# MoE layer: each token's expert outputs added up in one DRAM row by accumulating indirect stores, the last two experts' outputs kept on chip, and the order of the last products changed

## The chip, the cores and the metric

The kernel runs on one core of a Trainium2 chip. The metric is the device time of one execution in microseconds (us). The core has a matrix engine (TensorE, "PE" in the profile, its weight loads "PEld"), VectorE ("DVE"), ScalarE ("ACT"), GpSimd ("POOL") and SyncE ("SP"), which issues most of the transfers, and 16 DMA engines that carry them out.

## What is computed

One decoder layer on 512 tokens of width 1024: two token mixers in parallel, a merge, a layer norm, and then a grouped mixture of 16 experts with a second layer norm. The change is in the mixture alone:

```
def grouped_moe(x, w_router, b_router, w_gate, w_up, w_down):
    gates = shared_group_router(xt, w_router, b_router)   # two experts of 16 for each token
    out = jnp.zeros_like(xt)
    for e in range(N_EXPERTS):
        h = jax.nn.silu(xt @ w_gate[e]) * (xt @ w_up[e])  # 1024 -> 512
        out = out + gates[:, e:e + 1] * (h @ w_down[e])   # 512 -> 1024
    return out
...
x = layer_norm(DN_ALPHA * x + moe, ln2_g[l], ln2_b[l])
```

Weights and activations are float32. The kernel splits each operand of a product into a high part in the matrix engine's reduced float32 format and the remainder, and multiplies high by high, low by high and high by low.

## The kernel before

The program has one instruction stream for each engine, written out by hand, with semaphores between them. The first 540 us are the mixers, the first norm (which leaves `x1`, 512 rows in on-chip memory) and the router. The router picks two experts for each token and makes lists: for expert `b`, `lists[:, b, :]` holds up to 128 entries of (token, row in `ys`, gate). An entry that no token fills is (512 + p, 1024 + p, 0) for its place p. Tokens beyond 128 for one expert would go to further blocks in a loop `more`; no expert has as many here, and that loop doesn't run.

Then the experts come one after the other; call them 0 to 15 (`NE` = 16). For each, as the code names the steps:

- SP loads 6 MB of weights in six transfers of 1 MB (`load_expert`, L371) into six buffers `est0` to `est5`: two halves of the gate weights, two of up, two of down. A transfer is issued when VectorE has read the expert before out of that buffer (semaphores `gu_lo`, `d_lo`).
- ScalarE rounds a buffer to its high part (`e_round`, L1124, `ehi<-est`), and VectorE takes the remainder (`e_rest`, L1490, `elo<-est,ehi`). They are what the matrix engine reads, so a load may run one expert ahead.
- GpSimd gathers the expert's tokens from `x1d` in DRAM (`gather`, L550, `xe<-x1d,lists`). The entries of other tokens, over `bounds_check`, move nothing.
- TensorE in `turn(b)`: `gate_up(b)`, 48 matmuls (L841 to L843) in four parts, the first two into `psA[0]`, the others into `psA[1]`; `rows_t(b+1)`, 8 transposes of the next expert's tokens (L825); `down(b-1)`, 24 matmuls into `psB` in two parts (L866 to L868); `hidden_t(b)`, 4 transposes of the hidden rows (L852).
- ScalarE takes silu of `psA[0]`, VectorE multiplies it by `psA[1]` (`hidden`, L1717, `hb`), and the two split the transposed result (L1190, L1721, `hT_lo`).
- ScalarE scales the expert's output by the gates out of `psB` into `yb` (`y_out`, L1198), and GpSimd stores its rows to `ys` in DRAM (`scatter`, L557). `ys` has 1024 rows, two for each token, so that no two experts write one row. The `bounds_check` leaves unfilled entries out.

Expert 15's output isn't stored: it stays on chip as `last_hi` and `last_lo` (L1251, L1784), and a 0/1 matrix `last_by` puts its rows in the tokens' places by a matmul. At the end the order on TensorE is `gate_up(15)` parts 0 and 1, `down(14)`, `gate_up(15)` parts 2 and 3, `hidden_t(15)`, `down(15)`. SP loads both rows of each token (`yg<-ys`, L500, eight transfers of 512 KB) when every store has landed, GpSimd adds `x1` to one of them (L604), and for each of four tiles `t` of 128 tokens TensorE adds the two rows (L941, float32 matmuls by the identity) and expert 15's (L948) in `pairs[t]`. VectorE takes the second norm (`summed(t)`: moments L1534 and variance; `rstd(t)`; `scale_rows(t)`: L1561, L1563), and SP stores the tile.

## Time and profile before

| | |
|---|---|
| median of 3 runs | 845.21 us (844.38 to 845.37) |
| the profiled execution, device time | 846.67 us |
| its span in the trace | 845.0 us |
| TensorE busy | 823.1 us (97%) |
| VectorE, ScalarE, GpSimd busy | 572.6 us, 452.6 us, 74.5 us |
| granted TensorE clock over the span | 0.992 |

The span is what the trace covers, and the device time has 1.67 us more around it. "PEclk" is the TensorE clock that was granted, in parts of full speed (1.00 is 2.4 GHz, 0.50 is 1.2 GHz). The matrix engine pipelines, so a matmul's row is longer than the step from one to the next.

### The profile page before, as it was taken

How to read it: one execution, taken by the hardware profiler on the slowest of the kernel's cores; microseconds unless marked ns; L12 is line 12 of the kernel's file. 1: busy time of each engine (PE TensorE's matmuls, PEld its weight loads, DVE VectorE, ACT ScalarE, POOL GpSimd, SP SyncE). 2: the span in 40 equal slices, each digit the busy share in tenths (PEclk: the TensorE clock that was granted, in tenths of full speed). 3: DMA queues.
4: the chain of work that ended last, by engine and by line, in shares of the span. 5: the costliest groups of instructions: out<-in, count | busy, mean ns of one | idle time of the engine just before them, and what ended most of it. 6: DMA issues, size and time to landing. Idle time of an engine off the chain costs nothing.

```text
span 845.0 us, 11135 instructions
## 1 busy us (share of the span) xinstructions
PE 823.1 (97%) x3825; PEld 681.0 (81%) x3825; DVE 572.6 (68%) x658; ACT 452.6 (54%) x458; POOL 74.5 (9%) x74
## 2 busy tenths in 40 slices
PE   9999999999999999999999999999999999999984
PEld 9788788888888888888888888887888888888752
DVE  4887434434457885422456688879998889999547
ACT  4565434434466664332232333668788788886620
POOL 1000000100000000000000000822001111110140
PEclk9999999999999999999999999999999999999997
DMA  7233234553233333334533925799999999999552
GB/s 208 81 106 98 77 98 151 192 181 99 75 99 99 99 100 100 99 100 128 158 87 105 343 93 232 221 377 403 399 390 389 387 390 379 387 386 389 201 218 99
DMA packets 112338, 173.76 MB, mean 206 GB/s; under 512 B 7455, under 2 KB 90056, under 8 KB 100534
## 3 DMA queue, kind: packets, MB, share of 16 engines
q1 hardware_dynamic: 106342, 159.80, 53.6%
q0 software_dynamic: 5968, 13.61, 4.5%
q8 instruction: 16, 0.26, 0.1%
q14 instruction: 12, 0.10, 0.0%
HBM read 163.49 MB, written 16.82 MB: 213 GB/s over the span
## 4 chain that ended last, share of the span: by engine, by line
PE 86%; DVE 7%; issue 3%; POOL 2%; ACT 2%; DMA 1%; DVEq 0%; ACTq 0%; POOLq 0%
PE psA L654 7%; PE psA L655 7%; PE psA L656 7%; PE psB L656 6%; PE psB L654 6%; PE psB L655 6%; PE psA L841 6%; PE psA L843 6%; PE psA L842 5%; PE psB L866 3%; PE psB L868 3%; PE psB L867 3%; PE psD L654 2%; PE psD L656 2%; PE psD L655 2%
## 5 line engine op out<-in xcount | busy, mean ns | idle before, releaser
L1490 DVE TENSOR_TENSOR elo<-est,ehi 128x2048 fp32r<-128x2048 f32 x96 | 214.9, 2286 | 29.7 <-ACT ehi L1124 29.2
L1124 ACT ACTIVATE ehi<-est 128x2048 fp32r<-128x2048 f32 x96 | 180.2, 1915 | 27.0 <-DMA est<-in_w_exp_down_dram 12.8
L1280 DVE TENSOR_TENSOR wlo<-wst,whi 128x1024 fp32r<-128x1024 f32 (+1 forms) x76 | 95.0, 1250 | 91.9 <-ACT whi L963 90.7
L963 ACT ACTIVATE whi<-wst 128x1024 fp32r<-128x1024 f32 (+1 forms) x76 | 81.8, 1077 | 71.6 <-PE psB L656 30.6
L841 PE MATMUL psA<-ehi,xe_hi 128*128 128x512 f32 x256 | 101.4, 396 | 0.9 <-DVE xe_lo L1709 0.5
L843 PE MATMUL psA<-ehi,xe_lo 128*128 128x512 f32 x256 | 99.9, 390 | 0.0
L842 PE MATMUL psA<-elo,xe_hi 128*128 128x512 f32 x256 | 99.7, 389 | 0.0
L654 PE MATMUL psB<-xT_hi,whi 128*128 128x512 f32 x208 | 81.0, 390 | 0.0
L656 PE MATMUL psB<-xT_hi,wlo 128*128 128x512 f32 x208 | 80.9, 389 | 0.0
L655 PE MATMUL psB<-xT_lo,whi 128*128 128x512 f32 x208 | 80.9, 389 | 0.0
L841 PEld LDWEIGHTS psA<-ehi,xe_hi 128*128 128x128 f32 x256 | 48.2, 188 | 10.6 <-issue 1.3
L843 PEld LDWEIGHTS psA<-ehi,xe_lo 128*128 128x128 f32 x256 | 48.1, 188 | 10.2
L842 PEld LDWEIGHTS psA<-elo,xe_hi 128*128 128x128 f32 x256 | 48.1, 188 | 9.4
L654 PE MATMUL psA<-xT_hi,whi 128*128 128x512 f32 (+1 forms) x144 | 55.3, 384 | 0.1
L655 PE MATMUL psA<-xT_lo,whi 128*128 128x512 f32 (+1 forms) x144 | 55.2, 383 | 0.0
L656 PE MATMUL psA<-xT_hi,wlo 128*128 128x512 f32 (+1 forms) x144 | 55.2, 383 | 0.0
L866 PE MATMUL psB<-ehi,hT_hi 128*128 128x512 f32 x128 | 52.0, 407 | 2.4 <-DVE hT_lo L1721 2.4
L868 PE MATMUL psB<-ehi,hT_lo 128*128 128x512 f32 x128 | 50.5, 395 | 0.0
L867 PE MATMUL psB<-elo,hT_hi 128*128 128x512 f32 x128 | 50.4, 394 | 0.0
L655 PEld LDWEIGHTS psB<-xT_lo,whi 128*128 128x128 f32 x208 | 39.0, 188 | 8.2
L656 PEld LDWEIGHTS psB<-xT_hi,wlo 128*128 128x128 f32 x208 | 39.0, 188 | 8.1
L654 PEld LDWEIGHTS psB<-xT_hi,whi 128*128 128x128 f32 x208 | 39.0, 188 | 8.0
(331 smaller groups left out, 1507.9 us busy)
## 6 DMA issues: line engine op xcount, KB each, us to landing
est<-in_w_exp_gate_dram SPq DMA_DIRECT2D x32, 1024.0 KB, 12.5
est<-in_w_exp_up_dram SPq DMA_DIRECT2D x32, 1024.0 KB, 10.6
est<-in_w_exp_down_dram SPq DMA_DIRECT2D x32, 1024.0 KB, 12.0
wst<-in_w_in_dram SPq DMA_DIRECT2D x60, 512.0 KB, 3.9
wst<-in_w_branch_r_dram SPq DMA_DIRECT2D x8, 640.0 KB, 4.4
ys<-zero POOLq DMA_DIRECT2D x8, 512.0 KB, 2.9
wst<-in_w_branch_a_dram SPq DMA_DIRECT2D x8, 512.0 KB, 3.5
o_st<-in_w_out_dram SPq DMA_DIRECT2D x8, 512.0 KB, 4.4
```

The costliest lines, as they stand in the source:

```text
L654: pe.matmul(bank, s_hi[:, k, :], m_hi[:, k, :], start=(k == 0), stop=False)
L655: pe.matmul(bank, s_hi[:, k, :], m_lo[:, k, :], start=False, stop=False)
L656: mm = pe.matmul(bank, s_lo[:, k, :], m_hi[:, k, :], start=False, stop=(k == K - 1))
L841: pe.matmul(psA[s // 2], x_hi[:, q, :], ehi[s][:, k, :], start=(q == 0), stop=False)
L842: pe.matmul(psA[s // 2], x_hi[:, q, :], elo[s][:, k, :], start=False, stop=False)
L843: mm = pe.matmul(psA[s // 2], x_lo[:, q, :], ehi[s][:, k, :], start=False, stop=(q == KD - 1))
L866: pe.matmul(psB[n], hT_hi[:, k, :], ehi[4 + s][:, at_k, :], start=(k == 0), stop=False)
L868: mm = pe.matmul(psB[n], hT_lo[:, k, :], ehi[4 + s][:, at_k, :], start=False, stop=(k == KF - 1))
L963: A(whi[p][:, 0:K, :], wst[p][:, 0:K, :], ACT.Copy).then_inc(w_hi, 1)
L1124: A(ehi[s][:], est[s][:], ACT.Copy).then_inc(gu_hi if s < 4 else d_hi, 1)
L1280: V.tensor_tensor(wlo[p][:, 0:K, :], wst[p][:, 0:K, :], whi[p][:, 0:K, :], ALU.subtract).then_inc(w_lo, 1)
L1490: V.tensor_tensor(elo[s][:], est[s][:], ehi[s][:], ALU.subtract).then_inc(gu_lo if s < 4 else d_lo, 1)
```

## The change

Five things are changed. (1) `ys` has one row a token (640 rows with 128 spare ones), and each store to it adds to what stands there (`compute_op=ALU.add`). It goes by the token, column 0 of the list, has no `bounds_check` any more, and waits for the store before it to have landed. Of the zeroing stores to `ys` five are left of eight. (2) Expert 14's output stays on chip too, as `prev_hi`, `prev_lo`, with matrices `prev_by`. (3) The order of TensorE's last products is another one, and `down(15)` becomes `last_down` with weight and hidden buffers of its own, into `psA`. (4) The four tiles of `ys` are loaded, and `x1` is added to them, as soon as expert 13's store has landed, and the second norm's constants are loaded behind them. (5) In the sums of tile `t`, expert 14's matmuls come first, then one row a token by the identity, then expert 15's; VectorE finishes tile 0 before it starts on tile 1.

```diff
-    ys = nc.dram_tensor("ys", (ROWS + P, D), F32, kind="Internal").ap()
+    ys = nc.dram_tensor("ys", (S + P, D), F32, kind="Internal").ap()
...
+            sp.wait_ge(y_stored[0], (NE // 2 - 1) * 16)
+            sp.wait_ge(y_stored[1], (NE // 2 - 2) * 16)
+            sp.wait_ge(more_stored, 16)
+            sp.wait_ge(gu_used, 4 * NE - 3)
+            for t in range(TT):
+                load_pair(t, got[t])
...
+            sp.wait_ge(gu_used, 4 * NE)
+            sp.wait_ge(more_stored, more * 16 + 16)
             for n, v in enumerate((ln2_g, ln2_b)):
                 sp.dma_start(ln2_gb[:, n, :], v.to_broadcast([P, D])).then_inc(ln2_landed, 16)
...
             def scatter(b, idx):
 
                 pool.wait_ge(y_evac, b * 2 + 2)
+                if b > 0:
+                    pool.wait_ge(y_stored[(b - 1) % 2], ((b - 1) // 2 + 1) * 16)
                 pool.indirect_dma_start(out=ys, out_offset=bass.IndirectOffsetOnAxis(ap=idx, axis=0),
-                                        in_=yb[b % 2][:], in_offset=None, bounds_check=ROWS - 1,
-                                        oob_is_err=False).then_inc(y_stored[b % 2] if b < NE - 2 else more_stored, 16)
+                                        in_=yb[b % 2][:], in_offset=None, compute_op=ALU.add
+                                        ).then_inc(y_stored[b % 2] if b < NE - 3 else more_stored, 16)
...
                 if b >= 4:
-                    scatter(b - 4, lists[:, b - 4, 1:2].bitcast(U32))
-            for b in range(NE - 4, NE - 1):
-                scatter(b, lists[:, b, 1:2].bitcast(U32))
+                    scatter(b - 4, lists[:, b - 4, 0:1].bitcast(U32))
+            for b in range(NE - 4, NE - 2):
+                scatter(b, lists[:, b, 0:1].bitcast(U32))
+            for t in range(TT):
+                pool.wait_ge(got[t], 16)
+                nc.gpsimd.tensor_tensor(yg[t][:], yg[t][:], x1[:, t, :], ALU.add).then_inc(pre_done, 1)
...
+            gate_up(NE - 1)
+            down(NE - 2, parts=range(1))
             hidden_t(NE - 1)
-            down(NE - 1)
+            down(NE - 2, parts=range(1, 2))
+            last_down()
...
+            pe.wait_ge(last_listed, 2)
+            pe.wait_ge(last_l, 2)
+            for t in range(TT):
+                if t == 2:
+                    pe.wait_ge(y_evac, NE * 2)
+                    pe.wait_ge(last_l, 4)
+                by_prev(t)
+                pe.wait_ge(pre_done, t + 1)
+                for h in range(2):
+                    pe.matmul(pairs[t][:, h, :], ident[:], yg[t][:, h * S:(h + 1) * S], start=False, stop=False)
+                by_last(t)
...
+            act.wait_ge(gu_lo, 4 * NE)
+            act.wait_ge(e_landed[4], NE * 16)
+            A(dl_hi[0][:], est[4][:], ACT.Copy).then_inc(d_hi, 1)
+            act.wait_ge(h_t, NE)
+            act.wait_ge(y_stored[0], (NE // 2 - 1) * 16)
+            A(h15_hi[:], psC[1][:, 0, :].rearrange("p (k c) -> p k c", c=P), ACT.Copy).then_inc(h_h, 1)
+            act.wait_ge(e_landed[5], NE * 16)
+            A(dl_hi[1][:], est[5][:], ACT.Copy).then_inc(d_hi, 1)
...
             for t in range(TT):
-                if t + 1 < TT:
+                if 0 < t < TT - 1:
                     summed(t + 1)
                 rstd(t % 2, 1, TT + 1 + t)
...
+                if t == 0:
+                    summed(1)
```

How rows of the instruction streams move is shown at two places. The first is VectorE behind the last expert of the loop, with the semaphores each row waits for. Before, expert 15's first half of the down weights (`elo_188`) comes ahead of `hb`, the product of expert 15's hidden rows:

```order
L1775 TENSOR_SCALAR last_by<-slots,keys 128x128 x3
L1490 TENSOR_TENSOR elo_188<-est_176,ehi_182 128x2048 [waits d_hi]
L1717 TENSOR_TENSOR hb<-sg,psA 128x512 [waits h_t,gu_used,silu_done]
L1721 TENSOR_TENSOR hT_lo<-psD,hT_hi 128x512 [waits h_h]
L1490 TENSOR_TENSOR elo_189<-est_177,ehi_183 128x2048 [waits d_hi]
L1784 SCALAR_TENSOR_TENSOR last_lo<-psB,lists,last_hi 128x512 [waits y_evac] x2
```

After, in the same place, with expert 14's matrices and remainders added:

```order
L1826 TENSOR_SCALAR prev_by_217<-slots,keys 128x128
L1831 TENSOR_TENSOR dl_lo_208<-est_176,dl_hi_206 128x2048 [waits d_hi]
L1767 TENSOR_TENSOR hb<-sg,psA 128x512 [waits h_t,gu_used,silu_done]
L1844 TENSOR_TENSOR h_lo<-psD,h_hi 128x512 [waits h_h]
L1831 TENSOR_TENSOR dl_lo_209<-est_177,dl_hi_207 128x2048 [waits d_hi]
L1836 SCALAR_TENSOR_TENSOR prev_lo<-psB,lists,prev_hi 128x512 [waits y_evac] x2
L1836 SCALAR_TENSOR_TENSOR last_lo<-psA,lists,last_hi 128x512 [waits y_evac] x2
```

The product `hb` still stands behind the first half of expert 15's down weights, and it now follows all of `gate_up(15)`; the weights go to buffers of their own. The second place is TensorE's last products: the rows at which it waits, from the second half of `gate_up(15)` on. Before:

```order
L866 MATMUL psB<-ehi_182,hT_hi 128x512 [waits d_lo,y_evac,h_l]
L866 MATMUL psB<-ehi_183,hT_hi 128x512 [waits d_lo]
L841 MATMUL psA<-ehi_180,xe_hi 128x512 [waits gu_lo,h_done,xe_l]
L841 MATMUL psA<-ehi_181,xe_hi 128x512 [waits gu_lo]
L852 MATMUL psD<-ident,hb 128x128 [waits h_l,h_done]
...
L941 MATMUL psC<-yg,ident 128x512 [waits pre_done]
L948 MATMUL psC<-last_hi,last_by 128x512 [waits last_l,last_listed]
```

After:

```order
L859 MATMUL psA<-ehi_181,xe_hi 128x512 [waits gu_lo]
L884 MATMUL psB<-ehi_182,hT_hi 128x512 [waits d_lo,y_evac,h_l]
L870 MATMUL psD<-ident,hb 128x128 [waits h_l,h_done]
L884 MATMUL psB<-ehi_183,hT_hi 128x512 [waits d_lo,y_evac,h_l]
L945 MATMUL psA<-dl_hi_206,h_hi 128x512 [waits d_lo,h_l]
L945 MATMUL psA<-dl_hi_207,h_hi 128x512 [waits d_lo]
...
L971 MATMUL psC<-prev_hi,prev_by_214 128x512 [waits last_l,last_listed]
L992 MATMUL psC<-yg_220,ident 128x512 [waits pre_done]
L979 MATMUL psC<-last_hi,last_by 128x512 [waits last_l]
```

`down(14)` has moved behind all of `gate_up(15)` and stands around expert 15's transposes, `last_down` follows it directly, and the wait for the rows from DRAM (`pre_done`) comes behind four matmuls that don't need it.

## Rows read from the trace of the kernel before

**Rows 1.** The page: busy time, and the slices of TensorE and DMA.

```profile
PE 823.1 (97%) x3825; PEld 681.0 (81%) x3825; DVE 572.6 (68%) x658; ACT 452.6 (54%) x458; POOL 74.5 (9%) x74
...
DMA  7233234553233333334533925799999999999552
```

**Rows 2.** Window, one expert's turn: busy PE, PEld, DVE, ACT, POOL; clock, DMA, GB/s.

```profile
700.00:717.70 17.70, 17.70 (x85) 14.86 (x84) 15.76 (x10) 14.20 (x11) 2.22 (x2) 1.00 0.98 389
```

**Rows 3.** DMA queues and issues in 740:757.7, one expert's turn.

```profile
q1 hardware_dynamic: 863, 6.28, 91.0%
q0 software_dynamic: 288, 0.55, 8.1%
...
est<-in_w_exp_gate_dram SPq DMA_DIRECT2D x2, 1024.0 KB, 13.1
```

**Rows 4.** Short windows: a full one, and the emptiest of a turn.

```profile
749.00:750.50 1.50, 1.50 (x9) 1.23 (x8) 1.32 (x1) 1.50 (x2) 0.00 (x0) 1.00 1.02 431
752.00:753.50 1.50, 1.50 (x9) 1.24 (x9) 1.50 (x1) 1.25 (x2) 0.00 (x0) 1.00 0.91 273
```

**Rows 5.** Timeline of DVE and PE: expert 15's gate weights, and their first use.

```profile
776.35 4.48 DVE L1490 TENSOR_TENSOR elo<-est,ehi 128x2048 fp32r<-128x2048 f32 x2
...
787.49 0.48 PE L841 MATMUL psA<-ehi,xe_hi 128*128 128x512 f32 x1
```

**Rows 6.** Timeline of PE: the last products and tile 0's sum.

```profile
792.82 0.39 PE L843 MATMUL psA<-ehi,xe_lo 128*128 128x512 f32 x1
794.24 0.50 PE L866 MATMUL psB<-ehi,hT_hi 128*128 128x512 f32 x1 [1.02 <-DVE hT_lo L1721]
...
799.81 0.39 PE L841 MATMUL psA<-ehi,xe_hi 128*128 128x512 f32 x1
...
805.02 0.39 PE L843 MATMUL psA<-ehi,xe_lo 128*128 128x512 f32 x1
806.25 0.75 PE L852 MATMUL psD<-ident,hb 128*128 128x128 f32 x4 [0.83 <-DVE hb L1717]
808.41 0.80 PE L866 MATMUL psB<-ehi,hT_hi 128*128 128x512 f32 x1 [1.41 <-DVE hT_lo L1721]
...
815.43 3.59 PE L941 MATMUL psC<-yg,ident 128*128 128x512 f32 x8
818.46 0.79 PE L948 MATMUL psC<-last_hi,last_by 128*128 128x512 f32 x1
...
819.78 3.59 PE L941 MATMUL psD<-yg,ident 128*128 128x512 f32 x8
```

**Rows 7.** Window in which TensorE starts again.

```profile
808.00:810.00 2.00, 1.59 (x4) 1.31 (x5) 2.00 (x2) 0.00 (x0) 0.00 (x0) 0.54 0.96 389
```

**Rows 8.** Timeline of SP and POOL behind the loop: loads, store, adds.

```profile
773.79 20.15 SPq L371 DMA_DIRECT2D est<-in_w_exp_down_dram  x4
...
792.48 1.96 POOL L557 DMA_INDIRECT ys<-yb,lists  x1 [15.78 <-ACT yb L1198]
...
810.68 4.91 POOL L604 TENSOR_TENSOR yg<-yg,x 128x1024 f32<-128x1024 f32 x2 [7.66 <-DMA yg<-ys]
```

**Rows 9.** DMA issues in 783:800, then 792:815; us to landing last.

```profile
est<-in_w_exp_down_dram SPq DMA_DIRECT2D x2, 1024.0 KB, 6.2
...
ys<-yb,lists POOLq DMA_INDIRECT x1, 9.4
...
yg<-ys SPq DMA_DIRECT2D x8, 512.0 KB, 6.6
```

**Rows 10.** Timeline of DVE: last remainders and the second norm.

```profile
816.41 1.41 DVE L1784 SCALAR_TENSOR_TENSOR last_lo<-psB,lists,last_hi 128x512 fp32r<-128x512 f32 x2 [5.86 <-ACT last_hi L1251]
820.06 1.29 DVE L1534 BATCH_NORM_STATS2 stat<-psC 128x6 f32<-128x512 f32 x2 [2.24 <-PE psC L948]
...
824.34 1.30 DVE L1534 BATCH_NORM_STATS2 stat<-psD 128x6 f32<-128x512 f32 x2 [2.55 <-PE psD L948]
...
840.70 1.29 DVE L1563 SCALAR_TENSOR_TENSOR yg<-yg,stat,ln_gb 128x1024 f32<-128x1024 f32 x1
```

More of the change, by code:

```diff
@@ L486, in _ @@
             with sp.If(more > 0):
+                sp.wait_ge(d_used, 2 * NE)
                 with sp.Fori(0, more) as i:
@@ L541, in _ @@
             pool.dma_start(x1d[S:S + P, :], zero[:]).then_inc(trash_zeroed, 16)
-            for n in range(2 * TT):
+            for n in range(TT + 1):
                 pool.wait_ge(tile_done, 21 + n)
@@ L854, in hidden_t, with down @@
                 mm.then_inc(h_t, 1)
-            def down(b, first=False):
+            def down(b, first=False, parts=range(2)):
                 pe.wait_ge(h_l, b + 1)
@@ L859, in down @@
                     pe.wait_ge(y_evac, b * 2)
-                for s in range(2):
+                for s in parts:
                     pe.wait_ge(d_lo, b * 2 + (s + 1))
@@ L918, in _, with last_down @@
             turn(NE - 2, 1, xe_landed[1], NE // 2 * 16)
-            gate_up(NE - 1, parts=range(2))
-            down(NE - 2)
-            gate_up(NE - 1, parts=range(2, 4))
+            def last_down():
+                pe.wait_ge(h_l, NE)
+                for s in range(2):
+                    pe.wait_ge(d_lo, NE * 2 - 1 + s)
+                    for q in range(2):
+                        k = 2 * s + q
+                        for n in range(2):
+                            at_k = 2 * q + n
+                            pe.matmul(psA[n], h15_hi[:, k, :], dl_hi[s][:, at_k, :], start=(k == 0), stop=False)
+                            pe.matmul(psA[n], h15_hi[:, k, :], dl_lo[s][:, at_k, :], start=False, stop=False)
+                            mm = pe.matmul(psA[n], h15_lo[:, k, :], dl_hi[s][:, at_k, :], start=False,
+                                           stop=(k == KF - 1))
+                    mm.then_inc(d_used, 1)
+            gate_up(NE - 1)
+            down(NE - 2, parts=range(1))
             hidden_t(NE - 1)
-            down(NE - 1)
+            down(NE - 2, parts=range(1, 2))
+            last_down()
             pe.wait_ge(plan_done, 2)
@@ L950, in _ @@
                 mm.then_inc(sum_done, 1)
+            pe.wait_ge(last_listed, 2)
+            pe.wait_ge(last_l, 2)
+            for t in range(TT):
+                if t == 2:
+                    pe.wait_ge(y_evac, NE * 2)
+                    pe.wait_ge(last_l, 4)
+                by_prev(t)
[3 more added lines that the diff above has]
+                by_last(t)
         @block.scalar
@@ L1768, in _ @@
             dve.wait_ge(lists_landed, 16)
-            token, tail = keys[:, 0, :], keys[:, 1, :]
-            chain.link(V.tensor_copy(token[:, 0:1], lists[:, NE - 1, 0:1]))
-            for t in range(TT):
-                ins = V.tensor_scalar(tail[:, t:t + 1], token[:, 0:1], -float(t * P), None, ALU.add)
-            chain.link(ins)
-            for t in range(TT):
-                ins = V.tensor_scalar(last_by[:, t * P:(t + 1) * P], slots[:], tail[:, t:t + 1], None, ALU.is_equal)
-            ins.then_inc(last_listed, 1)
@@ L1777, in _, with placed, last_weights @@
-            e_rest(NE - 1, 4)
+            def placed(e, token, tail, out):
+                chain.link(V.tensor_copy(token, lists[:, e, 0:1]))
+                for t in range(TT):
+                    ins = V.tensor_scalar(tail[:, t:t + 1], token, -float(t * P), None, ALU.add)
+                chain.link(ins)
+                for t in range(TT):
+                    ins = V.tensor_scalar(out(t), slots[:], tail[:, t:t + 1], None, ALU.is_equal)
+                ins.then_inc(last_listed, 1)
+            def last_weights(n):
+                dve.wait_ge(d_hi, NE * 2 - 1 + n)
+                V.tensor_tensor(dl_lo[n][:], est[4 + n][:], dl_hi[n][:], ALU.subtract).then_inc(d_lo, 1)
@@ new lines, in remainder @@
+            def remainder(ps, e, y_hi, y_lo, s, count):
+                dve.wait_ge(y_evac, count)
+                half = slice(s * DF, (s + 1) * DF)
+                V.scalar_tensor_tensor(y_lo[:, half], ps[s], lists[:, e, 2:3].bitcast(F32),
+                                       y_hi[:, half], ALU.mult, ALU.subtract).then_inc(last_l, 1)
+            placed(NE - 1, keys[:, 0, 0:1], keys[:, 1, :], lambda t: last_by[:, t * P:(t + 1) * P])
+            placed(NE - 2, keys[:, 0, 1:2], keys[:, 2, :], lambda t: prev_by[t][:])
@@ L1786, in _ @@
+            for s in range(2):
+                remainder(psA, NE - 1, last_hi, last_lo, s, NE * 2 - 1 + s)
             dve.wait_ge(plan_done, 2)
@@ L1797, in _ @@
                     hidden_rest(b)
+                dve.wait_ge(got_again, TT * 16)
+                for t in range(TT):
+                    V.tensor_tensor(yg[t][:], yg[t][:], x1[:, t, :], ALU.add).then_inc(again_done, 1)
             dve.wait_ge(ln2_landed, 32)
```

83 lines of the change are left out of this document (41 added, 42 removed).

## The prediction

> **What bounds the kernel now.** I read the page's slices first. TensorE is busy for 97% of the span, and the DMA engines, at a third before the experts, are at nine tenths from there to the last loads [rows 1]. The second view is the windows cut to one expert's turn: TensorE is busy in all 17.70 us at the full clock, and the 16 DMA engines have a share of 0.98 with 389 GB/s [rows 2]. So two resources are full at once, and the question is which has room. The queues say what fills the DMA engines: the weight loads 91.0%, GpSimd's gather and store together 8.1% for 0.55 MB [rows 3]. A load of 1 MB takes 13.1 us to land [rows 3], while at 389 GB/s it is 2.7 us of work: four or so stand in the queue at any time. Short windows show what is spare: a full one moves 431 GB/s at a share of 1.02, the emptiest of a turn has 0.91 [rows 4], which is (1.02 - 0.91) x 1.5 = 0.17 us. I take 0.3 us a turn as spare, with smaller gaps elsewhere.
>
> TensorE waits for no load, since the work is ahead of it: VectorE ends expert 15's first gate quarter at about 776.35 + 2.2 = 778.6, and TensorE starts on it at 787.49 [rows 5]. That lead, 8.9 us, is what late loads may use up before TensorE stands.
>
> Behind the loop TensorE does stand: 1.2 us before `down(14)`, 1.0 us before the transposes, 1.4 us before `down(15)` [rows 6], which then starts at a clock of 0.54 of full speed [rows 7], the lower of the two levels for most of that window. From 820.06 on VectorE sets the pace, with a wait of 2.55 us for the second tile [rows 10].
>
> **The end, if the loop stays as it is.** From 787.49:
> - `gate_up(15)` in one piece: its halves take 792.82 + 0.23 - 787.49 = 5.56 and 805.02 + 0.23 - 799.81 = 5.44 us [rows 6], so it ends at 798.5. The wait of 1.2 us goes, since `down(14)`'s hidden rows are ready at 794.2.
> - First part of `down(14)`: 12 matmuls, a quarter of 11.0, 2.7 us: 801.2.
> - The transposes need `hb`, which stands on VectorE behind the first half of expert 15's down weights. SP issues that load between 773.79 and 793.94, the last but one of four [rows 8]; one step of 2.2 us before the last is 791.4. The two of that window land after 6.2 us, the mean of both [rows 9], and this one meets an emptier queue than the other: I take 5 us, 796.4, and 7.4 us for the other, 801.0 (issued at 793.6). Rounding 1.9 and remainder 2.2 us (half of 4.48 [rows 5]) lead to 800.6, `hb` 0.7 more: 801.3. So it about meets the transposes. They take 0.7: 802.1.
> - Second part of `down(14)` 2.7: 804.8. It covers the splitting of expert 15's hidden rows (808.41 - 807.0 = 1.4 us of standing before [rows 6]), and the second half of the weights: landed at 801, rounded behind the hidden rows by 804.7, remainder at 807. The last part of the products starts at 807.5, so that cover has 0.5 us left.
> - `last_down` 5.4: 810.2. Before, this point was 815.43 [rows 6]. 5.2 us come from the three waits (3.6) and the slow clock (the rest).
> - Tile 0's sum: expert 14's four matmuls 0.9, the identity's four records 4/8 x 3.03 = 1.5 (815.43 to 818.46), expert 15's four 1.0: 813.6. The first two cover the last remainders, which end 816.41 + 1.41 - 815.43 = 2.4 us behind the products [rows 10]. VectorE starts 0.3 later: 813.9, before 820.06.
> - The norm: from 820.06 to 842.0 is 21.9 us; the wait of 2.55 for the second tile goes, as tile 0 is finished meanwhile, and ScalarE's root for tile 0, some 0.4 us, is now in the open: 19.8. End 833.7, and 3.0 for the last store as before: span **836.7**, 8.3 less than 845.0.
>
> This needs the rows from DRAM in time. Expert 13's store is issued at 792.48 [rows 8] and takes 9.4 us [rows 9]: 801.9. The first tile's load then takes 3 to 4 us by my estimate (eight together took 6.6 [rows 9]), the add 2.4: about 808, and TensorE asks for it at 811.1. So the store may be 3 us slower at no cost; behind that each us is lost. The other adds follow at 2.4 us each, faster than VectorE's 4.8 us a tile. Fewer zeroing stores and the added matrices for expert 14 (1.4 us on an idle VectorE) cost nothing; GpSimd's new wait for the store before is hidden too, with 17.7 us between stores and 9.4 for one. The gather queued behind it has then that slack as well.
>
> **The loop: the accumulating stores.** Nothing in the trace accumulates. The nearest rows are the gather and the plain store: 0.55 MB is 134 rows of 4 KB, and 8.1% of 17.7 us is 1.43 us of all engines, so 0.0107 us a row, 0.72 us for a store of some 67 rows. Without `bounds_check` the unfilled entries are stored as well: 128 rows. If an added row costs what a plain one does, a store is 1.37 us, 0.65 more than now. If the engine has to fetch the old row as a gather does and store it as a store does, it is both at once: 2.74 us, **2.0 more**. I take the second, since the row must be read from DRAM and its addend from on-chip memory, and the engines are full, so that nothing can be hidden beside. Above, a row that waits for its old contents before the next one starts might cost half as much again, 4.1 us, 3.4 more. Below the plain price nothing is reasonable.
>
> The Trainium skill, "Collectives: The Full Stack", section "The bandwidth ceiling: the fold count and why AG ≠ RS ≠ AR", speaks against the change in the same way: a reducing transfer is not slowed by the addition but by reading two sources through one ring, with a measured ratio of 1.93 between copying and reducing. By it a store would cost 1.93 x 1.37 = 2.6 us, an estimate, and the sum below would be 1.2 us lower. No row here shows it.
>
> Twelve stores (0 to 11) fall before expert 15's gate weights land. Each adds 2.0, of which 0.3 is spare: 12 x 1.7 = 20.4 us of lateness, less the lead of 8.9: TensorE stands 11.5 us in all, spread over the later experts. 836.7 + 11.5 = 848.2 of span. The profiled execution's 846.67 stands 1.67 over its span, and the median of the runs, 845.21, is 0.2 over the span; so I forecast **848** for the median. The break is at a lateness of 17.2 us, 1.73 more a store: a store price of 2.45 us. My value is close above it, which is why the chances are near even.
>
> **Rivals.**
> - *Added rows at the plain price.* 12 x (0.65 - 0.3) = 4.2 us of lateness, within the lead. TensorE never stands, and the end's gain is whole: 837. For it: reading and writing are two sides of one transfer, and a second read might go in parallel. Against it: both rows are read from somewhere, and the engines show no gap. Any price up to 0.3 + 8.9/12 = 1.04 more gives the same. 34 in 100. This is the other side.
> - *My forecast*, 1.4 to 2.7 more a store: 842 to 855. 42 in 100.
> - *Each row waits for its old contents*: 3.4 more, 12 x 3.1 - 8.9 = 28 us: 865. 14 in 100, from 855 up.
> - *The loop holds, and the end is late*: the accumulating store of expert 13, with 128 rows beside the last two loads, lands 5 to 8 us later than 801.9. Then the first tile's rows, and the norm's constants queued behind them, come 2 to 5 us late: 839 to 842. 10 in 100.
>
> **How the numbers follow.** A difference of 0.2%, 1.7 us, is about what a measurement of this kernel tells from none: 843.5 to 846.9. Faster: 0.32 of the first, 0.05 of the second's lower end, 0.09 of the last: 0.45 or so. Same: 0.08 of the second and a little of the others, 0.10. Slower: the rest, 0.45. The range reaches from the plain price, 836, to the lower part of the third case, 861.
>
> **What would show it.** The windows of one turn: longer than 17.75 us at a DMA share of 1, with TensorE below full, if I am right; 17.75 with TensorE full by the first rival. In the waits, PE idle behind `elo` (VectorE), and ScalarE behind `est` loads, growing over the experts. Software queue share per turn: 8.1% would go to 12% at the plain price and 20% at mine. `gate_up(15)` in one piece and about 0.2 us before the transposes shows the end's first steps; the first norm row 3.7 us behind the last product, and 4.8 us a tile from there, the others. The forecast fails if the record prices the added rows under 2.45 us.

## The result, and the profile after

The changed kernel takes **856.43 us** (median of 4 runs, 855.63 to 857.15) against 844.98 (844.38 to 845.37) beside it: ratio 1.0124, 95% interval 1.0108 to 1.0141, slower. The profiled execution took 855.63 us, with a span of 854.0. The forecast was 848 with a range of 836 to 861: the direction and what bounds the loop hold, and the size is 8 us short. By the spans the change costs 9.0 us, by the medians 11.4: the execution profiled before was 1.7 us above its kernel's median, the one after 0.8 below.

The page of the changed kernel, busy time, DMA slices and bytes in GB/s (compare [rows 1]):

```profile
PE 824.1 (97%) x3825; PEld 681.5 (80%) x3825; DVE 575.5 (67%) x669; ACT 453.1 (53%) x458; POOL 92.5 (11%) x70
...
DMA  7232325533333333335425644999999999999762
GB/s 213 77 115 82 98 75 162 191 92 98 99 98 98 97 89 109 97 88 158 139 72 193 263 177 160 296 362 394 399 378 369 367 359 362 378 375 379 252 219 98
```

TensorE's busy time is 1.0 us above that of before although the span is 9.0 longer. The nine tenths of the DMA engines last a slice longer, and they move less: 359 to 399 GB/s, where the page of the kernel before has 377 to 403 and a turn had 389 [rows 2]. A window of one turn's usual length, from an expert's first gate matmul on, answers to [rows 2] and [rows 3]: busy PE, PEld, DVE, ACT, POOL, then clock, DMA share and GB/s; below it queues and issues of the same stretch, with us to landing last:

```profile
704.50:723.70 19.20, 18.26 (x84) 14.94 (x84) 15.57 (x9) 14.26 (x12) 4.46 (x2) 1.00 1.02 366
```

```profile
q1 hardware_dynamic: 856, 6.23, 84.4%
q0 software_dynamic: 287, 0.78, 17.2%
...
est<-in_w_exp_gate_dram SPq DMA_DIRECT2D x2, 1024.0 KB, 13.9
ys<-yb,lists POOLq DMA_INDIRECT x1, 12.8
xe<-x1d,lists POOLq DMA_INDIRECT x1, 13.2
```

The turns here are 19.05 to 19.45 us long, where they were 17.76, with the DMA engines full (1.02) and TensorE busy for 18.26 of 19.2. (It stands 0.94 by the rows; the other 0.5 of the 1.44 doesn't show, since a matmul's row goes on for 0.16 us beyond the step to the next.) GpSimd's queue takes 17.2% of 19.2 = 3.30 us of all engines; less 0.72 for the gather (half of the prediction's 1.43), a store costs **2.58 us**. Who waited over the experts, in us in total, times and the longest, in 560 to 800. Before:

```profile
DVE elo L1490 <- ACT ehi L1124: 14.4, 20, 4.7
...
ACT ehi L1124 <- DMA est<-in_w_exp_down_dram: 9.3, 12, 1.5
```

After:

```profile
ACT ehi L1167 <- DMA est<-in_w_exp_down_dram: 46.7, 23, 2.8
DVE elo L1540 <- ACT ehi L1167: 40.2, 37, 4.3
...
ACT ehi L1167 <- DMA est<-in_w_exp_up_dram: 8.2, 11, 2.0
...
PE psA L859 <- DVE xe_lo L1759: 4.7, 11, 0.5
...
PE psB L884 <- DVE hT_lo L1771: 3.5, 8, 0.7
```

ScalarE waits 46.7 us for down weights, VectorE behind it, and TensorE for VectorE's `xe_lo` and `hT_lo`. VectorE's timeline ahead of expert 15's start:

```profile
793.04 4.49 DVE L1540 TENSOR_TENSOR elo<-est,ehi 128x2048 fp32r<-128x2048 f32 x2 [0.54 <-ACT ehi L1167]
797.46 0.68 DVE L1767 TENSOR_TENSOR hb<-sg,psA 128x512 f32<-128x512 f32 x1
798.05 1.22 DVE L1759 TENSOR_TENSOR xe_lo<-psC,xe_hi 128x1024 fp32r<-128x1024 f32 x1
```

TensorE's from there on:

```profile
799.32 0.50 PE L859 MATMUL psA<-ehi,xe_hi 128*128 128x512 f32 x1
...
816.74 0.75 PE L870 MATMUL psD<-ident,hb 128*128 128x128 f32 x4 [3.48 <-DVE hb L1767]
...
821.67 0.40 PE L945 MATMUL psA<-dl_hi,h_hi 128*128 128x512 f32 x1
```

And ScalarE's, with the roundings of expert 14's down weights, the output of expert 13 and the first of expert 15's down weights:

```profile
802.71 1.92 ACT L1167 ACTIVATE ehi<-est 128x2048 fp32r<-128x2048 f32 x1 [2.44 <-DMA est<-in_w_exp_down_dram]
805.18 1.92 ACT L1167 ACTIVATE ehi<-est 128x2048 fp32r<-128x2048 f32 x1 [0.55 <-DMA est<-in_w_exp_down_dram]
807.00 0.58 ACT L1233 ACTIVATE hT_hi<-psD 128x512 fp32r<-128x512 f32 x1
807.47 1.26 ACT L1241 ACTIVATE yb<-psB,lists 128x512 f32<-128x512 f32 x2
...
811.85 1.91 ACT L1288 ACTIVATE dl_hi<-est 128x2048 fp32r<-128x2048 f32 x1 [2.62 <-DMA est<-in_w_exp_down_dram]
```

Expert 15's gate product starts at 799.32, when `xe_lo` has ended (799.27): 11.83 us later than 787.49 [rows 5]. The second thing to see is that TensorE stands 3.48 us before the last transposes. VectorE's timeline at the end:

```profile
813.79 2.29 DVE L1831 TENSOR_TENSOR dl_lo<-est,dl_hi 128x2048 fp32r<-128x2048 f32 x1 [1.08 <-ACT dl_hi L1288]
816.00 0.68 DVE L1767 TENSOR_TENSOR hb<-sg,psA 128x512 f32<-128x512 f32 x1
...
830.98 1.29 DVE L1584 BATCH_NORM_STATS2 stat<-psC 128x6 f32<-128x512 f32 x2 [1.44 <-PE psC L979]
...
849.62 1.29 DVE L1613 SCALAR_TENSOR_TENSOR yg<-yg,stat,ln_gb 128x1024 f32<-128x1024 f32 x1
```

SP's and then POOL's, with the last loads, the store of expert 13 and the adds (compare [rows 8]):

```profile
806.99 2.81 SPq L380 DMA_DIRECT2D est<-in_w_exp_down_dram  x2
818.28 1.76 SPq L494 DMA_DIRECT2D yg<-ys  x4
821.17 0.34 SPq L516 DMA_DIRECT2D ln_gb<-in_ln_g_dram  x1
821.55 0.43 SPq L516 DMA_DIRECT2D ln_gb<-in_ln_b_dram  x1
...
809.01 1.84 POOL L575 DMA_INDIRECT ys<-yb,lists  x1 [15.69 <-ACT yb L1241]
822.16 9.44 POOL L605 TENSOR_TENSOR yg<-yg,x 128x1024 f32<-128x1024 f32 x4 [11.31 <-DMA yg<-ys]
```

From the first gate matmul of expert 15 to the end of the span it is 845.0 - 787.5 = 57.5 us before and 854.0 - 799.3 = 54.7 after. So 11.8 us are lost in the loop and 2.8 won behind it, together the 9.0 of the spans.

### The profile page after: what moved, and what is told of

Same layout as the page of the kernel before. It is cut to its first block, busy times and chain, and to the rows that moved or that the text cites. A ratio compares the mean times of both kernels' runs of the same rounds, so it can differ in the third digit from the quotient of the medians.

```text
span 854.0 us, 11134 instructions
## 1 busy us (share of the span) xinstructions
PE 824.1 (97%) x3825; PEld 681.5 (80%) x3825; DVE 575.5 (67%) x669; ACT 453.1 (53%) x458; POOL 92.5 (11%) x70
## 3 DMA queue, kind: packets, MB, share of 16 engines
HBM read 161.39 MB, written 14.73 MB: 206 GB/s over the span
## 4 chain that ended last, share of the span: by engine, by line
PE 60%; DMA 22%; DVE 9%; ACT 4%; issue 3%; POOL 2%; SPq 0%; DVEq 0%; ACTq 0%; POOLq 0%
DMA est<-in_w_exp_down_dram 21%; PE psA L672 7%; PE psA L674 7%; PE psA L673 7%; PE psB L672 6%; PE psB L674 6%; PE psB L673 6%; DVE elo L1540 4%; ACT ehi L1167 3%; PE psD L672 2%; PE psD L674 2%; PE psD L673 2%; POOL tab L590 2%; PE psC L674 1%; PE psC L672 1%
## 5 line engine op out<-in xcount | busy, mean ns | idle before, releaser
L1540 DVE TENSOR_TENSOR elo<-est,ehi 128x2048 fp32r<-128x2048 f32 x94 | 212.3, 2287 | 48.5 <-ACT ehi L1167 48.5
L673 PE MATMUL psA<-xT_lo,whi 128*128 128x512 f32 (+1 forms) x144 | 55.2, 383 | 0.0
L674 PE MATMUL psA<-xT_hi,wlo 128*128 128x512 f32 (+1 forms) x144 | 55.2, 383 | 0.0
L884 PE MATMUL psB<-ehi,hT_hi 128*128 128x512 f32 x120 | 48.8, 407 | 3.5 <-DVE hT_lo L1771 3.5
L886 PE MATMUL psB<-ehi,hT_lo 128*128 128x512 f32 x120 | 47.7, 397 | 0.0
L885 PE MATMUL psB<-elo,hT_hi 128*128 128x512 f32 x120 | 47.4, 395 | 0.0
L575 POOL DMA_INDIRECT ys<-yb,lists x14 | 25.8, 1845 | 184.7 <-ACT yb L1241 184.4
```

What stands on the lines that cost most here:

```text
L673: pe.matmul(bank, s_hi[:, k, :], m_lo[:, k, :], start=False, stop=False)
L674: mm = pe.matmul(bank, s_lo[:, k, :], m_hi[:, k, :], start=False, stop=(k == K - 1))
L884: pe.matmul(psB[n], hT_hi[:, k, :], ehi[4 + s][:, at_k, :], start=(k == 0), stop=False)
L886: mm = pe.matmul(psB[n], hT_lo[:, k, :], ehi[4 + s][:, at_k, :], start=False, stop=(k == KF - 1))
L1540: V.tensor_tensor(elo[s][:], est[s][:], ehi[s][:], ALU.subtract).then_inc(gu_lo if s < 4 else d_lo, 1)
```

## The experiments

Each kernel ran beside the one before on its chip, and is held against it by the ratio. The three groups of four runs had medians of before of 847.73, 847.96 and 847.01 us. "Turn" is the usual distance of TensorE's first gate matmuls in the middle of the loop, "gate 15" the start of expert 15's, "norm" the first row of the second norm, all from the timelines of one execution. The kernel before alone spreads over some 5 us in each group, so 2 us between two kernels of the table, 0.2%, are about what can't be told. The 0.327 us in the expectations is what an accumulated row of 4 KB took on its engine in the trace's packet records, and 0.159 us what a plain one took.

| kernel | turn | gate 15 | norm | span | median us | ratio (95%) |
|---|---|---|---|---|---|---|
| before | 17.76 | 787.5 | 820.06 | 845.0 | | 1 |
| changed | 19.2 | 799.3 | 830.98 | 854.0 | 856.43 | 1.0124 (1.0108 to 1.0141) |
| e2 plain stores | 17.76 | 788.2 | 815.13 | 837.8 | 839.56 | 0.9912 (0.9888 to 0.9935) |
| e1 bound | 18.6 | 795.0 | 826.13 | 849.1 | 851.17 | 1.0042 (1.0026 to 1.0059) |
| e5 80 entries | 18.0 | 787.7 | 815.56 | 838.5 | 840.37 | 0.9911 (0.9883 to 0.9939) |
| e10 80 and bound | 17.76 | 788.4 | 815.76 | 838.7 | 840.37 | 0.9918 (0.9894 to 0.9942) |
| e12 96 entries | 18.4 | 791.9 | 821.92 | 844.9 | 845.81 | 0.9980 (0.9965 to 0.9996) |
| e6 short load | 17.76 | 787.1 | 815.26 | 838.0 | 841.33 | 0.9930 (0.9902 to 0.9958) |
| e7 before, longer load | 18.6 | 798.1 | 834.32 | 859.3 | 860.94 | 1.0158 (1.0131 to 1.0185) |
| e3 order | 19.2 | 801.6 | 831.36 | 854.1 | 854.57 | 1.0068 (1.0042 to 1.0093) |
| e4 bound and order | 18.7 | 795.9 | 825.12 | 847.8 | 849.50 | 1.0020 (1.0006 to 1.0035) |
| e11 order, constants | 19.3 | 800.9 | 835.69 | 858.7 | 859.34 | 1.0142 (1.0111 to 1.0174) |
| e9 80, order, constants | 17.76 | 787.3 | 814.55 | 838.8 | 842.55 | 0.9957 (0.9943 to 0.9971) |
| e8 two rows, new end | 17.76 | 789.7 | 818.10 | 844.9 | 845.63 | 0.9973 (0.9957 to 0.9990) |

### What in the store costs

**e2**: everything of the change but the addition. Its output leaves one of a token's two experts out where both were stored. The expectations of e1 and e2 name the same two theories: the addition's engine time, or the new wait and the order of GpSimd's queue.

```diff
-                                        in_=yb[b % 2][:], in_offset=None, compute_op=ALU.add
+                                        in_=yb[b % 2][:], in_offset=None
```

> The changed kernel with plain stores instead of accumulating ones, 128 rows each, the wait for the store before kept; the second expert of a token then overwrites the first, so the output leaves one of them out. Theory 1: 128 rows at 0.159 us are 1.27 us of all engines, like e1: 17.75 us a turn and 837 to 839. Theory 2: the number of rows and the wait are those of the changed kernel, so turns near 19 us and 850 to 856.

Measured: 0.9912, with TensorE full in every turn. A window of one turn and its queues:

```profile
717.20:735.00 17.80, 17.80 (x88) 14.95 (x86) 15.86 (x10) 14.24 (x12) 3.13 (x2) 1.00 1.01 403
```

```profile
q1 hardware_dynamic: 870, 6.33, 89.4%
q0 software_dynamic: 293, 0.84, 11.8%
```

So it is theory 1: 128 plain rows a store, the wait for the store before, expert 14 on chip and the new order cost nothing together. What is lost is the addition's: 11.8% of 17.8 less 0.72 is 1.38 us for 128 plain rows, the prediction's 1.37, and 2.58 / 1.38 = 1.9. Over 160 us of both kernels (10.9% of 17.76 and 17.2% of 19.2, each less 0.72) it is 1.22 and 2.58, a factor of 2.1.

The Trainium skill gives a measured ratio of 1.93 between an all-gather, which copies, and a reduce-scatter, which adds ("Collectives: The Full Stack", "The bandwidth ceiling: the fold count and why AG ≠ RS ≠ AR"). This store isn't a collective, but the trace agrees with the ratio: 1.9 to 2.1.

**e1**: the bound on the indices is back, so that unfilled entries are left out of the accumulating store.

```diff
-                                        in_=yb[b % 2][:], in_offset=None, compute_op=ALU.add
+                                        in_=yb[b % 2][:], in_offset=None, compute_op=ALU.add,
+                                        bounds_check=S - 1, oob_is_err=False
```

> The changed kernel with one thing more: the accumulating store has bounds_check = 511 again, so that unfilled entries move nothing. Theory 1 (engine time of the added rows): in the changed kernel a row took 0.327 us on its engine, 128 rows 2.62 us of all 16. With some 64 rows a store is 1.3 us, 0.6 to 0.65 more than a plain store of before, 12 x (0.65 - 0.3) = 4 us of lateness within TensorE's lead of 8.9: a turn is 17.75 us again, TensorE never stands in the loop, and the end has its gain: 837 to 839. Theory 2 (the store's new wait for the one before it, or the gather queued behind accumulating rows, holds up TensorE): both are still there, so the turns stay over 18.5 us and the time near 850 to 856.

Measured: 1.0042, 12 us and more above theory 1. Half the rows should have brought the turn under TensorE's; it is 18.6 us. The time is the one that theory 2 named, but e2 has the same wait and loses nothing, so its reason isn't it.

```profile
q1 hardware_dynamic: 854, 6.21, 88.4%
q0 software_dynamic: 289, 0.55, 11.7%
```

GpSimd's queue is where it should be: 11.7% of 18.6 less 0.72 is 1.46 us, and half of 2.58 is 1.29. The packets are as many as with 128 rows (289), but 0.55 MB: a skipped entry isn't left out, it is a tiny packet (8 bytes in the packet records). The other queue has changed as well: 88.4% of 18.6 for 6.21 MB is 2.65 us for each MB of weights, where e2 has 89.4% of 17.8 / 6.33 = 2.51. That is 0.8 us more in a turn of 6.3 MB. e5 and e10 ask whether the skipped entries do it.

**e5**: the store takes the first 80 entries alone. The longest list here has 75 tokens, so all are stored; a longer list would lose tokens.

```diff
-                pool.indirect_dma_start(out=ys, out_offset=bass.IndirectOffsetOnAxis(ap=idx, axis=0),
-                                        in_=yb[b % 2][:], in_offset=None, compute_op=ALU.add
+                pool.indirect_dma_start(out=ys, out_offset=bass.IndirectOffsetOnAxis(ap=idx[0:80], axis=0),
+                                        in_=yb[b % 2][0:80], in_offset=None, compute_op=ALU.add
```

> The changed kernel with the accumulating store cut to its first 80 entries; no expert has more than 75 tokens, so nothing is left out. An accumulated row took 0.327 us of one DMA engine, so a store is 80 x 0.327 / 16 = 1.64 us of all 16, where the changed kernel has 2.62 and the run with a bound on the indices 1.31. Theory 1 (rows alone set the price): the engines have 1.64 - 0.72 = 0.92 us more to do in a turn than in the kernel before, 17.41 + 0.92 = 18.3, so a turn is 18.3 us or, by the 18.6 us that 1.31 us of rows gave with the bound, 18.9, and the run is slower than the one with the bound. Theory 2 (entries that the bound leaves out still cost, as 64 small packets that disturb the loads): a turn is 18.0 to 18.3 us, under the 18.6 of the bound although more rows are accumulated, and the time 843 to 848 us.

Measured: 0.9911, faster even than theory 2 had it, with 16 more rows added in a turn than e1.

```profile
716.10:734.10 18.00, 17.99 (x85) 14.97 (x85) 15.83 (x10) 14.20 (x12) 3.70 (x2) 1.00 1.02 391
```

```profile
q1 hardware_dynamic: 879, 6.40, 88.3%
q0 software_dynamic: 245, 0.63, 13.5%
```

Weights are at 88.3% of 18.0 / 6.40 = 2.48 us for each MB, 0.17 less than in e1. Single turns differ, though: over 160 us (620 to 780) it is 2.51 in e5 and 2.52 in e2 against 2.63 in e1, 0.8 us for a turn's 6.3 MB, and the changed kernel, which skips nothing, has 2.57. Theory 2 forecast the turn; what in the skipped entries does it is the next question.

**e10**: as e5, with e1's bound. **e12**: as e5, with 96 for 80.

> 80 entries and the bound on the indices together: some 64 rows are accumulated in a turn and 16 entries skipped, where the run with the bound alone skipped 64 and had turns of 18.6 us, and the one with 80 entries alone accumulated 80 rows and had 18.0. Theory 1 (a skipped entry costs about what the two runs give, (18.6 - 18.0 + 16 x 0.327 / 16) / 64 = 0.015 us of turn, as much as two thirds of an accumulated row): 18.0 - 0.33 + 0.24 = 17.9 us a turn, and 839 to 841 us. Theory 2 (the bound itself disturbs the loads, however many it skips): turns of 18.3 us and over, 845 us or more.

> The changed kernel with the accumulating store cut to 96 entries; nothing is left out. 96 x 0.327 / 16 = 1.96 us a store. The turns at 80 and 128 entries are 18.0 and 19.15 us, 0.024 us an entry. Theory 1 (the price is straight in the rows): 18.4 us a turn, 12 x (18.4 - 17.76) less a lead of 5.5 = 2.2 us later at expert 15's gate, and 842 to 844 us. Theory 2 (a step: beyond 80 rows something else fills up): turns of 19 us and 850 us or more.

Measured: e10 0.9918, the same as e5 (both 840.37 us), its turn TensorE's own 17.76: theory 1. So the bound itself costs nothing. e1 and e10 store the same rows and differ only in that e1 has 48 more entries to skip, and that is 18.6 against 17.76 us a turn and some 10 us.

The entries that are skipped hardly load the engines: 515 packets of 8 bytes with 0.009 us each in 160 us of e1, 0.03 us a turn. The packet records show something else: where the rows go. In e1 the 58 to 70 added rows of a store take 4.3 to 5.0 us from the first start to the last, as long as nearly all stores of 128 rows in the changed kernel (4.6 to 4.9, two of eight longer). They come in about eight chains, a row every 0.63 us in each (0.327 for the row, 0.309 for a packet of weights between), and at most 11 are under way at once, where the changed kernel has 16. The same rows in e10 take 2.7 to 4.2 us with up to 13 at once, as the 80 of e5 do (2.8 to 3.2).

The filled entries stand first in a list. So it looks as if a list is dealt out to the 16 engines in equal pieces: of 128 entries eight to each, so that some 64 rows all lie on half of the engines, which have 8 x 0.327 = 2.6 us of them, as much as in the changed kernel, while the others skip theirs; of 80 entries five to each, 1.6 us. The turns follow the fullest engine: 8 added rows on it 19.2 and 18.6 us, 6 (e12) 18.4, 5 (e5, e10) 18.0 and 17.76, and 8 plain ones, 1.3 us, 17.76 (e2 and the kernel before). If a load of weights lies on all engines alike, it lands with the fullest. This is read from the traces and not shown by a run: the records don't name the engine, and a list of 128 with its filled entries spread out was not tried.

e12's turn is 18.4 us as theory 1 said, but gate 15 comes 4.4 us later than before and not 2.2, and the time is 845.81, 2 us above what it said, ratio 0.998: 1.96 us a store is about the price at which the change pays nothing. The turn is straight in the rows: 18.0, 18.4 and 19.2 us at 80, 96 and 128, 0.025 us a row, a little more than the 0.327 / 16 = 0.020 of the engines' time.

### Is it the DMA engines' work, and how long is the lead

**e6**: the changed kernel, with half of each expert's second down load left out from expert 2 to 14 (the expectation says 3; the loop's last lines load the expert before). The products then use an earlier expert's weights there.

```diff
-            sp.dma_start(est[s][:], src).then_inc(e_landed[s], 16)
+            if s == 5 and again:
+                sp.dma_start(est[s][:, 0:2, :], src[:, 0:2, :]).then_inc(e_landed[s], 16)
+            else:
+                sp.dma_start(est[s][:], src).then_inc(e_landed[s], 16)
```

> The changed kernel with its accumulating stores whole, but the second half of each expert's down weights loaded only half from expert 3 to 14: 0.5 MB less in a turn, 1.3 us of all 16 engines by 0.159 us a row of 4 KB. The other half of those weights is that of an earlier expert, so the output isn't the reference's. Theory 1 (the engines' work in a turn is the bound): 19.2 - 1.3 = 17.9 us a turn, against TensorE's 17.65, so the lead is hardly used up and the time 837 to 842 us. Theory 2 (the store's additions hold back something else, such as the memory that the rows stand in or GpSimd): the turn stays over 18.5 us and the time over 850.

**e7**: the kernel before, with 0.5 MB more to load in a turn, and nothing that accumulates.

```diff
+            spare = at("spare", 162, [P, D])
+            spare_in = sem("spare_in")
+            sp.wait_ge(gu_used, 8)
+            sp.dma_start(spare[:], w_out[0, 0:P, :]).then_inc(spare_in, 16)
             with sp.Fori(3, NE) as b:
                 for s in range(4):
                     load_expert(sp, b, s, again=True)
+                sp.wait_ge(spare_in, b * 16 - 32)
+                sp.dma_start(spare[:], w_out[0, 0:P, :]).then_inc(spare_in, 16)
```

> The kernel before with one further load of 0.5 MB a turn from expert 3 on, into a buffer that nobody reads: 128 rows of 4 KB, 1.27 us of all engines, onto 17.41 in 17.63. It prices the lead alone, with no accumulation. 12 turns x (1.27 - 0.2) = 12.8 us of lateness. Theory A (the lead is the 8.9 us of the first gate quarter, as the prediction had it): TensorE stands 3.9 us more, 849. Theory B (the lead is 4.8 us, since the next tokens' splitting stands behind the rounding of the gate halves): 8 us more, 852 to 854. If it stays within 1 us of the kernel before, extra work of plain rows isn't what costs, and accumulation costs in another way.

Measured: e6 0.993, theory 1, its 128 added rows whole and TensorE full (17.70 of 17.70 us). With 1.3 us of other work taken out, the accumulation costs nothing, so neither GpSimd nor the rows' memory holds anything back. e7 1.0158: plain loads do the same harm. A window of e7:

```profile
705.60:724.40 18.80, 18.26 (x84) 14.96 (x84) 15.72 (x10) 14.13 (x12) 3.90 (x2) 1.00 0.98 386
```

TensorE is busy for 18.26 us of the turn, as in the changed kernel. The time is 7 to 9 us over what theory B said, 12 over theory A (3 of them are this chip's, where the kernel before took 847.96). Of the 14.3 us by which the span is longer than that of before (13.4 by the ratio), 2.7 are there when expert 4 starts (594.9 against 592.2), which may be the load in the first turns, or chance: e8 has 2.2 there without any such load; 7.9 come up to expert 15's start; the rest, 3.7, is the end, 61.2 us after gate 15 instead of 57.5. Both theories of the lead were too high for it.

The Trainium skill's page "DMA: Bandwidth & Descriptors", section "Issuing engines are not separate DMA queues", says that transfers that ScalarE, SyncE or GpSimd start run on the same 16 DMA engines and interleave. e6 agrees: less to load for SP makes room for GpSimd's store.

Where the lead went wrong can be read from the kernel before. VectorE's row for the next tokens' remainder:

```profile
782.88 1.22 DVE L1709 TENSOR_TENSOR xe_lo<-psC,xe_hi 128x1024 fp32r<-128x1024 f32 x1 [1.25 <-ACT xe_hi L1174]
```

TensorE's first gate matmul needs `xe_lo` too. It ends at 784.1, 3.4 us ahead of 787.49, while the gate quarter is 8.9 ahead. And on VectorE `xe_lo` stands behind both gate halves and `hb`, as the rows of after show, so that late weights make it late. By the turns: from expert 3's start to 14's it is 573.7 to 781.5 = 207.8 us in the changed kernel, 12.4 over 11 x 17.76; at 19.2 each it would be 15.8, so 3.4 us were covered. The same sum gives 2.6 for e12 and 2.0 for e1.

### The end

**e3**: `hb` ahead of the rounding remainder of expert 15's down weights.

```diff
-            last_weights(0)
             hidden(NE - 1)
+            last_weights(0)
```

> The changed kernel with two steps of VectorE exchanged: expert 15's product hb ahead of the remainder of the first half of its down weights. Theory A (what was lost at the end is hb standing behind weights that land late): the transposes come 3.3 us earlier, TensorE doesn't fall to the low clock, and the time falls by about 4.5 us to 852. Theory B (the end has a second limit just behind: the norm's constants are issued at 821.2 and 821.6, behind expert 13's store and the four tiles, and land by 830.7, and VectorE's first norm row waits for them and stands at 830.98): the products end earlier, the first norm row stays at 830.7, and the time falls by 0.5 us at most.

**e4**: e1 and e3 together.

> Both edits of e1 and e3. With the loads in time the first half of the down weights is ready before hb can be made, so the exchange should be worth 0 to 1 us over e1: 836 to 838. If e3's order matters even with the loads in time (theory A), 2 us or more below e1.

Measured: 1.0068 for e3, where the changed kernel had 1.0124 on another chip; that is 4.7 us by the ratios, 1.9 by the medians and nothing by the spans. e4 took 849.50 us, 1.0020, 11.5 above its expectation as e1 had missed its own, and 1.7 below e1 on the same chip. Counted from gate 15 to the end of the span, the two pairs agree: 54.7 us in the changed kernel and 52.5 in e3, 54.1 in e1 and 51.9 in e4. So the exchange is worth 2.2 us, half of what theory A gave for e3 and more than theory B's 0.5. In e3 the last product's remainders are there at 825.41, 2.7 us earlier than in the changed kernel, and the norm still starts at 831.36:

```profile
825.41 1.41 DVE L1836 SCALAR_TENSOR_TENSOR last_lo<-psA,lists,last_hi 128x512 fp32r<-128x512 f32 x2 [2.58 <-ACT last_hi L1300]
831.36 1.30 DVE L1584 BATCH_NORM_STATS2 stat<-psC 128x6 f32<-128x512 f32 x2 [4.54 <-DMA ln_gb<-in_ln_b_dram]
```

It waits 4.54 us for the norm's constants. They are queued on SP behind the tiles' rows, and those wait for expert 13's store. (In the changed kernel the last of them, issued at 821.55, lands after 9.1 us at 830.65, just ahead of the norm at 830.98.) That is theory B's second limit.

**e11**: e3, and the constants ahead of the rows. **e9**: the same with 80 entries.

```diff
-            sp.wait_ge(gu_used, 4 * NE - 3)
+            sp.wait_ge(gu_used, 4 * NE)
+            for n, v in enumerate((ln2_g, ln2_b)):
+                sp.dma_start(ln2_gb[:, n, :], v.to_broadcast([P, D])).then_inc(ln2_landed, 16)
             for t in range(TT):
                 load_pair(t, got[t])
```

> The changed kernel, all 128 entries accumulated, with the two edits of the end alone: the hidden rows' rounding ahead of the down weights', and the norm's constants loaded ahead of the tiles' rows. The first edit alone took 1.5 us off, and its first row of the norm still came at 831.4. Theory A (the constants, landing at 830.65 us, were the second limit): the first row of the norm at 827 to 829, and 852 to 854 us. Theory B (the tile's rows, late behind expert 13's store, or the down weights are the limit): 855 to 857, no better than with the rounding alone.

> The changed kernel with the accumulating store cut to 80 entries, the hidden rows' rounding ahead of the down weights', and the norm's constants loaded ahead of the tiles' rows. The run with 80 entries alone took 840.4 us; TensorE stood 1.34 us before the transposes of expert 15's hidden rows there, and nothing else over 0.25 us until the norm. Theory A (those 1.3 us are the last that the order can give): 838.5 to 839.5 us. Theory B (what is won there is lost again, because the second half of the down weights lands no earlier): 840 to 841, no gain over the run with 80 entries alone.

Measured: e11 1.0142 and 859.34 us, slower than e3 and above both theories, nearer to B. TensorE, SP and POOL in e11:

```profile
830.53 2.08 PE L992 MATMUL psC<-yg,ident 128*128 128x512 f32 x2 [5.16 <-POOL yg L605]
```

```profile
820.41 0.42 SPq L501 DMA_DIRECT2D ln_gb<-in_ln_b_dram  x1
820.88 2.35 SPq L494 DMA_DIRECT2D yg<-ys  x4
...
810.87 1.84 POOL L575 DMA_INDIRECT ys<-yb,lists  x1 [15.94 <-ACT yb L1241]
828.14 9.29 POOL L605 TENSOR_TENSOR yg<-yg,x 128x1024 f32<-128x1024 f32 x4 [15.44 <-DMA yg<-ys]
```

Now the rows come behind the constants, GpSimd adds 6 us later than in the changed kernel, and TensorE stands 5.16 us for them. So either order makes one of the two late. In e11 both still wait for expert 13's store; the constants ahead of that wait, with one row a token, were not tried. e9 took 842.55 us (840.43 to 845.43), 2.2 above e10 on the same chip and 1.5 above theory B's 841: no gain, and rather a loss. With the loop in time the order of the change is good enough.

**e8**: the end of e9, but two plain rows a token as in the kernel before, eight row loads and two identity products a tile.

> The changed kernel's order of the end, but with the kernel before's stores: two rows a token, each written by one plain store, both loaded at the end and added by TensorE; the norm's constants are loaded ahead of these rows, and the hidden rows' rounding stands ahead of the down weights'. Theory 1 (all of the loss is the accumulation, all of the gain is the order of the end): turns of 17.5 us, first row of the norm near 814 to 816, and 838 to 840 us, against 856 for the changed kernel and 845 for the one before. Theory 2 (the gain needs the single row, since four more loads and eight more products at the end are late): 841 to 844.

Measured: 0.9973 and 845.63 us, above both theories. 2.2 us are lost to the first turns (gate 15 at 789.7 with all later turns at 17.76), and the end is 844.9 - 789.7 = 55.2 us where e5 has 50.8:

```profile
810.91 2.39 POOL L607 TENSOR_TENSOR yg<-yg,x 128x1024 f32<-128x1024 f32 x1 [14.28 <-DMA yh<-ys]
```

GpSimd waits for the second rows until 810.91; in e5 it starts at 807.17. So the single row a token is worth some 4 us at the end (55.2 against 50.8 in e5 and 51.5 in e9), and accumulation pays, at 80 entries. The fastest versions that compute all, for lists of up to 80 tokens, are e5 and e10, 0.9911 and 0.9918 of the kernel before.

## Why the prediction was right in kind and short in size

- **The direction**: right, but "the chances are near even": faster and slower had 0.45 each. What decided it was the price of an added row.
- **What bounds the loop**: right. The DMA engines are full, TensorE waits for VectorE, VectorE for ScalarE, ScalarE for weights, and e6 and e7 show the engines' work as the cause from both sides. Only the last link is another one: TensorE waits for `xe_lo` (4.7 us) and `hT_lo` (3.5), not for `elo`.
- **The price of an added row**: right. Taken 2.74 us a store, measured 2.58; plain 1.37 taken, 1.38 measured. The "plain price" rival is out, and so is the one that waits for old contents. GpSimd's queue has 17.2% of a turn, where the prediction said 20.
- **Spare time**: 0.3 us a turn taken. A store is 2.58 - 0.72 = 1.86 us dearer and the turn 1.44 longer, so 0.4.
- **The lead**: wrong, "8.9 us, is what late loads may use up", by leaving `xe_lo` out. It is 3.4 at most.
- **Lateness at expert 15's gate**: 11.5 forecast, 11.83 measured. Two errors nearly cancel: 12 x 1.7 - 8.9 against 11 x 1.44 - 3.4 = 12.4, less 0.7 by which expert 3 had started earlier than before (573.7 against 574.4). The break-even store price has no such luck: 2.45 us forecast, about 1.96 by e12.
- **The end with the loop in time**: right. 836.7 - 787.5 = 49.2 us from expert 15's gate forecast; e2 has 49.6, e10 50.3, e5 50.8. (In e2 the first norm row waits 1.82 us for the norm's constants, which the sum hadn't counted.) The norm: 19.8 forecast, 830.98 to 850.91 = 19.9 measured, and 3.1 for the last store.
- **The end behind a late loop**: this is the step that failed, the 5.5 us by which 848.2 misses the span of 854.0 after the loop's 0.3. "The end, if the loop stays as it is" was shifted by 11.5 us as one block. But SP issues the first half of expert 15's down weights when VectorE has read expert 14's, and those were late themselves (ScalarE stood 2.44 us at 802.7). So it was issued at 806.99 and not at 791.4 + 11.8 = 803.2, ScalarE waited 2.62 us for it, and `hb`, behind it on VectorE, ended at 816.7 and not 801.3 + 11.8 = 813.1. TensorE stood 3.48 us, and then got the lower of its two clock levels, which cost another 1.4 us or so up to `last_down` (821.67, forecast 804.8 + 11.8 = 816.6). Windows of the changed kernel, clock third from the end:

```profile
814.00:816.00 2.00, 0.00 (x0) 0.00 (x0) 2.00 (x1) 0.00 (x0) 0.00 (x0) 1.00 0.96 207
816.00:818.00 2.00, 1.26 (x7) 1.12 (x8) 0.68 (x2) 0.48 (x1) 0.00 (x0) 0.93 0.45 88
818.00:820.00 2.00, 2.00 (x7) 1.51 (x6) 0.74 (x2) 1.92 (x2) 0.00 (x0) 0.50 0.37 88
```

- **From the span to the median**: "0.2 over the span" was taken from the kernel before, whose profiled execution was slower than its median. The changed kernel's median is 2.4 over its span, and this is the rest of the 8 us.
- **The rival "the loop holds, and the end is late"** named a real limit with a wrong condition: it comes with the late loop. Expert 13's store was issued at 809.01, 4.7 us later than 792.48 + 11.83, since ScalarE scales `yb` (807.47) behind the roundings that wait for weights. In the changed kernel this limit (the constants at 830.65) and the products (830.87) end together; e3 shows it by itself, at 831.36.

I had given the two causes chances as if they excluded each other, and they came together.

## What to carry to other kernels

Price an added row as two plain ones, count the rows on the engine that seems to have most of them, and cut the list to its length: 80 entries instead of 128 turned 1.2% slower into 0.9% faster, while skipping the unfilled ones of 128 won only part of it (0.4% slower). Before a lead is counted, look up every operand of the waiting instruction and what stands ahead of each on its engine; the least lead counts. And don't shift the end of a kernel as a block: once loads bound the loop, whatever hangs on the last loads slips by more than the loop did.

## What was not expected of the hardware

- Entries that `bounds_check` skips still are packets, of 8 bytes in the accumulating store and 0.009 us. They cost nearly nothing themselves, but a list with many of them doesn't free the engines as expected: the added rows of e1 are carried out by about half of the engines at a time (at most 11 at once, 4.3 to 5.0 us for some 64 rows), and the weights' loads beside them cost 2.63 us for each MB against 2.51 in e5. That the long list does it rests on e1 against e10; how is read from the packet records alone. In plain stores the same is small: over 160 us, 91.2% for 57.15 MB in the kernel before and 89.9% for 57.16 MB in e2, 0.2 us a turn of 6.3 MB.
- The page's count of DRAM traffic doesn't show the old contents: "HBM read 161.39 MB" stands in the page of the changed kernel and in that of e2 alike, though the added rows take twice the time of the plain ones. Such a store can't be found by its bytes, only by its queue's share.
